# Two transformer blocks on one core: Pool's modulation sums in one block, a log-term buffer per head, spatial products between the z projections

## The chip, the core and the metric

The kernel runs on one core of a Trainium2 chip. Its engines are called here by the profile's names: PE (TensorE, the matrix unit; PEld its weight loads), DVE (VectorE), ACT (ScalarE), POOL (GpSimd) and SP (SyncE, which issues the weight loads from memory). The metric is the device time of one execution in microseconds, the median of several. Before the change it is 2369.49 us (three runs, 2369.08 to 2371.31).

## The reference

The program computes two transformer blocks in a row on 512 positions of width 1024, in float32. Only what the change touches:

```
c_act = silu(c);  mod = c_act @ w_ada + b_ada        # 9 vectors of 1024: 0,1,2 | 3,4,5 | 6,7,8
u = rmsnorm(x, g1) * (1 + mod[1]) + mod[0]           # first norm
h = x + 0.5 * mod[2] * swiglu(u)                     # FFN1, hidden width 2816
u = rmsnorm(h, g2) * (1 + mod[4]) + mod[3]           # second norm
y = mixer(u)      # short convolution, stick-breaking attention with 8 heads, gated merge, w_out
h = h + mod[5] * y
u = rmsnorm(h, g3) * (1 + mod[7]) + mod[6]           # third norm
h = h + 0.5 * mod[8] * swiglu(u)                     # FFN2, then a final norm

# stick-breaking attention, for each head and block of queries, strictly causal:
z = q @ k.T / 8;  sp = softplus(z);  rem = suffix sum of sp, without itself
a = exp(log_sigmoid(z) - rem);  o = a @ v

# second block, its spatial gating: 8 groups of 128 columns, 4 blocks of 128 positions
a = gelu(z_u) * (W_s[group] @ layernorm(gelu(z_v)) + b_s)
merged = gate_a * (a @ w_branch_a) + gate_b * (forgetting_attention @ w_branch_b)
```

## The kernel before

Activations stand transposed, as eight tiles of 128 features x 512 positions. Each operand of a dense product is split into a high part and a low rest, and each product is three matmuls (L448 high x high, L449 low x high, L450 high x low). A weight chunk is at most 8 tiles of 128 x 128: SP loads it into one of four slots (`raw`), ACT copies the high part (`split`, L837, `wh`), DVE subtracts to get the rest (`split`, L1216, `wl`), PE uses it (`dense`: 24 matmuls for 8 tiles). `split` runs three chunks ahead of PE, and SP reloads a slot when DVE has done its split. All engines run their own list of instructions in order; semaphores with counted values join them. The order of the lists is written out by hand.

**The modulation.** Vectors 0 and 1 are multiplied and added up by DVE itself at the start (L1582, L1586), PE sums over the partitions with a column of ones (L724, 32 pieces of one column, as a float32 product takes two passes), and DVE adds the bias (`modulation`, L1269) and makes the norm's gain (L1276). The other seven vectors are POOL's. For each vector it takes eight rows of tiles of `w_ada` through a ring of two buffers (`load`, L1774, 512 KB each, issued from POOL's own queue), multiplies by the column of `c_act` (L1786, L1788) and adds to `ada_acc` (L1792). There are only two accumulators, so POOL works in groups, each of which waits until PE has reduced the one before: vectors 2 and 3 after the first reduction, 4 and 5 after the first half of FFN1, 6 and 7 after the last head of the first attention (`o_lo`), since only then is the place free, and 8 after the reduction behind the output projection `out1`. `ada_reduce` on PE (L535) comes between the halves of FFN1 (2 and 3), after FFN1 (4 and 5), after `out1` (6 and 7) and between the halves of FFN2 (8).

**The norms.** PE sums squares with `mean_square` (L487), ACT takes the root, DVE inverts it (L1234), waits for the modulation, and then works tile by tile: DVE scales (L1252), ACT makes the high part (L867), DVE the rest (L1262), and PE starts a pair of dense products on each tile as it comes (`dense_pair`, 48 matmuls). FFN1 and FFN2 run in two halves (12 and 10 hidden tiles), each an up part (24 or 20 chunks of 8 tiles) and a down part (16 chunks of 6 or 5).

**The first attention** handles four pairs of heads (`body`, once per pair in each engine's list). For each head PE makes the scores z in PSUM (L546 to L549), and ACT three log terms into the buffer `x0`: |z| (L962), its exponential (L964) and the logarithm (L966). DVE makes the softplus (L1412), four suffix sums into `x1` (L1422) and the log weights back into `x0` (L1429), ACT the probabilities (L973). PE turns them (L558, `turn_probs`), ACT and DVE split them (L990, L1448, `turned_hi`, `turned_lo`), PE multiplies by the values (L573, L574). `x0` is shared by the two heads, so in ACT's list head 0's probabilities stand before head 1's log terms, which wait for them. Between these steps PE makes the projections of the next pair, and DVE's list has the weight splits, `q_lo` (L1360) and `k_lo` (L1367) of the next pair.

After it come four convolution tiles (`conv_in`, L1609 to L1621 on DVE), the merge (eight tiles, each two gates and two branches), and `out1`.

**The spatial gating of the second block** runs over eight groups m. DVE normalises the group (`normal_group`, L1672 to L1680), ACT and DVE split it (L1162, L1689), POOL masks the group's spatial weights, PE turns them (`turn_w`, L764) and makes 12 narrow matmuls (`mix_group`). DVE adds the bias (L1697) and multiplies with z (L1702), ACT and DVE split the result (L1167, L1704). PE also makes eight z projections (`z_in`, 24 matmuls), two of which fit in PSUM; ACT empties one (`z_out`, L1147) only when DVE has used the one two before, and `z_in` m waits for `z_out` m - 2. In PE's list `z_in(m + 4)` follows `mix_group(m)` for m = 0 to 3; the groups 4 to 6 follow with nothing between; then come the two gates of the merge's first tile and the last group:

```
            for m in range(DT - 1):
                turn_w(m + 1)
                mix_group(m // 4, m % 4)
                if m + 4 < DT:
                    z_in(m + 4)
```

Of the kernel before, what the change touches and what calls it, by code (L numbers as in the profile page):

```python
# [23 lines left out]
P = 128  # L24
# [56 lines left out]
def build(nc, a, out):  # L81
# [3 lines left out]
    with ctx:  # L85
# [58 lines left out]
        ada_acc = place("ada_acc", [P, 2 * D], F32, ada_at)  # L144
        ada_ring = place("ada_ring", [P, 4 * S], F32, ada_at + 4 * row)
# [23 lines left out]
        t1["x"] = place("x1", [P, 2 * PACK], F32, at)  # L169
        assert at + 8 * PACK <= ada_at  # L170
# [274 lines left out]
        def _(pe):  # L445
# [82 lines left out]
            def ada_reduce(group):  # L528

                count = 1 if group == 3 else 2  # L530

                pe.wait_ge(ada_add, 8 * (2 * group + count))
                for v in range(count):
                    for m in range(DT):
                        x = pe.matmul(bank(6, v * DT + m, 1), ada_acc[:, v * D + m * P:v * D + (m + 1) * P],  # L535
                                      one_col[:, :], start=True, stop=True, skip_group_check=True)
                x.then_inc(ada_red, 1)
# [116 lines left out]

            def merge(name, xa, xb, kt, ready_a, ready_b):
                nb, n0 = AT_[name], DT * ORDER[name]

                def gates(m):
                    for s, free in enumerate((MG["sa"], MG["sb"])):

                        pe.wait_ge(free, m + (n0 + 1))
                        if name == "merge2":
                            pe.wait_ge(G["z"], DT + 1 + s)
                        dense(nb + s, 4 * m, s, DT, uh, ul)
# [7 lines left out]
                gates(0)  # L672
                if name == "merge2":

                    mix_group(DT // 4 - 1, 3)
# [45 lines left out]
            pe.wait_ge(ada0, 16)  # L721
            for v in range(2):
                for m in range(DT):
                    mm = pe.matmul(bank(6, v * DT + m, 1), ada_acc[:, v * D + m * P:v * D + (m + 1) * P],  # L724
                                   one_col[:, :], start=True, stop=True, skip_group_check=True)
            mm.then_inc(ada_red, 1)

# [3 lines left out]
            ada_reduce(1)  # L731
# [17 lines left out]
            ada_reduce(2)  # L749
# [79 lines left out]
        def _(act):  # L829
# [79 lines left out]
            def attention(name, t, kind, pairs):  # L909
# [58 lines left out]
                def probabilities(p, hh):  # L968
                    pr = hh * PACK
                    if kind == 1:  # L970

                        act.wait_ge(A_["s_free"], 2 * p + (hh + 2))
                        act.activation(t["pr"][:, pr:pr + PACK], t["x"][:, 0:PACK], ACT.Exp).then_inc(A_["p"], 1)  # L973
# [236 lines left out]
        def _(dve):  # L1210
# [26 lines left out]
            def norm(q, k, gain, shift):  # L1237
# [27 lines left out]
            def modulation(n, v0, count):  # L1265
# [3 lines left out]
                dve.tensor_tensor(mods[:, v0 * DT:(v0 + count) * DT], bank(6, 0, count * DT),  # L1269
# [24 lines left out]
            def ffn(f, conv, gate):  # L1294
                s_, q, n0, r0 = F, RES_ROUND[f], FT * ORDER[f], DT * ORDER[f]
                for part, ((j0, tiles, kts), (gb, db)) in enumerate(zip(FFN_PARTS, chunks[f])):
# [37 lines left out]
                    if part == 0 and f == "ffn1":  # L1334
                        modulation(2, 2, 2)
                        half_gate(0, M_G0, 2)
                    if part == 0 and f == "ffn2":
                        modulation(5, 8, 1)
                        half_gate(2, M_G2, 5)
# [13 lines left out]
            def attention(name, t, kind, pairs):  # L1353
# [54 lines left out]
                def softplus(p, hh):  # L1408

                    x0, z = t["x"][:, 0:PACK], bank(B_HEAD[hh], 0, PACK)  # L1410
# [467 lines left out]
```

## Time and profile before

| | |
|---|---|
| median of three runs | 2369.49 us (2369.08 to 2371.31) |
| the profiled execution | 2372.86 us, its span 2371.2 us |
| PE busy | 2134.6 us, 90% of the span |
| DVE, ACT, POOL busy | 1305.7, 860.4, 308.2 us |
| mean granted PE clock | 0.937 of full speed |

The profile is of one execution. Times inside it count from the first instruction. PE's granted clock has two levels, 1.0 (2.4 GHz) and 0.5 (1.2 GHz), and a mean between them over a stretch is a mixture. Matmuls overlap: a dense matmul is shown with some 390 ns, but one follows the other every 227 to 235 ns at full clock and every 427 at half. Of POOL's times the page says that they are rough.

### The profile page before, as it was taken

The page shows a single profiled execution, that of the slowest core. Times are in us where ns is not written, and L with a number is a line of the kernel's source. Part 1 is how long each engine was busy: PE and PEld are TensorE (multiplying, and loading weights), DVE is VectorE, ACT ScalarE, POOL GpSimd, SP SyncE. Part 2 cuts the span into 40 slices and gives each one's busy share as a digit, 9 for nine tenths or more (in the row PEclk, how much of TensorE's full clock was granted, in tenths as well). Part 3 has the DMA queues.
Part 4 walks back from the last instruction along what each step waited for, and adds up shares of the span by engine and source line. Part 5 has one row for each costly group of instructions (what it writes and reads, how often), then busy time and mean ns, then how long its engine had stood idle before and what let it go on. Part 6 is the DMA issues. An engine that isn't in the chain of part 4 may idle for free.

```text
span 2371.2 us, 28854 instructions
## 1 busy us (share of the span) xinstructions
PE 2134.6 (90%) x9417; PEld 1752.2 (74%) x9417; DVE 1305.7 (55%) x1537; ACT 860.4 (36%) x1228; POOL 308.2 (13%) x222
## 2 busy tenths in 40 slices
PE   2799999887869997999996899997999989999967
PEld 2688888776647875888885688875788778888856
DVE  6844444666596448333346666666433466546554
ACT  2222223365414332222233556562222244334433
POOL 0843810000183006000000000011000000000000
PEclk6899999898879997999998899997899989999979
DMA  7453642221144333323323122233233322333212
GB/s 260 139 154 101 192 128 76 79 62 53 45 138 137 106 98 98 89 84 111 88 79 90 54 62 71 71 71 71 71 94 92 98 71 88 92 104 91 86 54 80
DMA packets 371706, 226.81 MB, mean 96 GB/s; under 512 B 8052, under 2 KB 361672, under 8 KB 370632
## 3 DMA queue, kind: packets, MB, share of 16 engines
q1 hardware_dynamic: 362248, 193.66, 27.8%
q0 software_dynamic: 9408, 32.51, 5.1%
q8 instruction: 28, 0.46, 0.1%
q14 instruction: 22, 0.18, 0.0%
HBM read 224.05 MB, written 2.10 MB: 95 GB/s over the span
## 4 chain that ended last, share of the span: by engine, by line
PE 80%; DVE 11%; ACT 4%; issue 4%; DVEq 0%; DMA 0%; ACTq 0%
PE ps L448 25%; PE ps L449 25%; PE ps L450 25%; DVE wl L1216 1%; PE ps L558 1%; DVE tmp L1252 1%; DVE x L1422 1%; PE ps L535 1%; DVE inv L1234 1%; PE ps L546 1%; PE ps L573 1%; PE ps L574 1%; PE ps L547 1%; DVE ssq L1229 1%; PE ps L487 1%
## 5 line engine op out<-in xcount | busy, mean ns | idle before, releaser
L448 PE MATMUL ps<-uh,wh 128*128 128x512 f32 x1896 | 764.2, 403 | 104.7 <-DVE ul L1262 36.7
L449 PE MATMUL ps<-ul,wh 128*128 128x512 f32 x1896 | 755.6, 399 | 0.0
L450 PE MATMUL ps<-uh,wl 128*128 128x512 f32 x1896 | 753.5, 397 | 0.0
L1216 DVE TENSOR_TENSOR wl<-raw,wh 128x1024 fp32r<-128x1024 f32 x389 | 531.2, 1369 | 248.2 <-ACT wh L837 240.5
L448 PEld LDWEIGHTS ps<-uh,wh 128*128 128x128 f32 x1896 | 366.8, 193 | 191.9 <-issue 63.5
L837 ACT ACTIVATE wh<-raw 128x1024 fp32r<-128x1024 f32 x389 | 408.7, 1052 | 223.3 <-PE ps L450 213.7
L450 PEld LDWEIGHTS ps<-uh,wl 128*128 128x128 f32 x1896 | 366.5, 193 | 79.1
L449 PEld LDWEIGHTS ps<-ul,wh 128*128 128x128 f32 x1896 | 367.0, 194 | 75.0
L448 PE MATMUL ps<-ah,wh 128*128 128x512 f32 x528 | 209.6, 397 | 0.0
L450 PE MATMUL ps<-ah,wl 128*128 128x512 f32 x528 | 209.2, 396 | 0.0
L449 PE MATMUL ps<-al,wh 128*128 128x512 f32 x528 | 209.1, 396 | 0.0
L1327 DVE TENSOR_TENSOR prod<-sq,ps 128x512 f32<-128x512 f32 x44 | 30.3, 688 | 278.2 <-PE ps L450 277.0
L1792 POOL TENSOR_TENSOR ada_acc<-ada_acc,ada_ring 128x1024 f32<-128x1024 f32 x49 | 138.9, 2835 | 3.8
L901 ACT ACTIVATE ah<-prod 128x512 f32 x66 | 41.8, 633 | 248.0 <-DVE prod L1327 248.0
L448 PEld LDWEIGHTS ps<-ah,wh 128*128 128x128 f32 x528 | 99.8, 189 | 23.9
L449 PEld LDWEIGHTS ps<-al,wh 128*128 128x128 f32 x528 | 99.8, 189 | 23.8
L450 PEld LDWEIGHTS ps<-ah,wl 128*128 128x128 f32 x528 | 99.7, 189 | 23.9
L1788 POOL TENSOR_TENSOR ada_ring<-ada_ring,cact 128x1024 f32<-128x1024 f32 x49 | 96.1, 1961 | 1.9 <-DMA ada_ring<-in_w_ada 0.9
L847 ACT ACTIVATE sq<-h 128x512 f32 x56 | 35.3, 631 | 158.6 <-DVE h L1292 89.4
L1786 POOL TENSOR_TENSOR ada_acc<-ada_ring,cact 128x1024 f32<-128x1024 f32 x7 | 13.7, 1951 | 598.3 <-DVE o1l L1504 336.7
L1851 POOL DMA_DIRECT2D ptok<-in_p x1 | 0.8, 807 | 626.7 <-DVE h L1290 626.7
L897 ACT ACTIVATE sq<-ps 128x512 f32<-128x512 f32 x44 | 26.3, 598 | 137.1 <-PE ps L450 137.1
(248 smaller groups left out, 2302.4 us busy)
## 6 DMA issues: line engine op xcount, KB each, us to landing
raw<-in_ffn_w_gu SPq DMA_DIRECT2D x88, 512.0 KB, 4.1
raw<-in_w_in SPq DMA_DIRECT2D x57, 512.0 KB, 3.8
ada_ring<-in_w_ada POOLq DMA_DIRECT2D x56, 512.0 KB, 4.1
raw<-in_w_up SPq DMA_DIRECT2D x44, 512.0 KB, 3.8
raw<-in_w_mix_in SPq DMA_DIRECT2D x40, 512.0 KB, 3.9
raw<-in_ffn_w_down SPq DMA_DIRECT2D x32, 384.0 KB, 3.2
raw<-in_ffn_w_down SPq DMA_DIRECT2D x32, 320.0 KB, 2.9
wada<-in_w_ada SPq DMA_DIRECT2D x8, 1024.0 KB, 12.7
```

Source lines behind the costliest of these rows:

```text
L448: pe.matmul(dst, lh, rh, start=first, stop=False, skip_group_check=True)
L449: pe.matmul(dst, lh, rl, start=False, stop=False, skip_group_check=True)
L450: return pe.matmul(dst, ll, rh, start=False, stop=last, skip_group_check=True)
L487: pe.matmul(bank(B_O), mean_w[:, :], ssq[:, :], start=True, stop=True).then_inc(ms_done, 1)
L837: act.activation(wh[:, w], raw[:, w], ACT.Copy).then_inc(w_hi, 1)
L847: act.activation(sq[:, r * S:(r + 1) * S], tile(h, m), ACT.Square).then_inc(sq_done, 1)
L897: act.activation(sq[:, buf], bank(2 * r), ACT.Silu).then_inc(s_["gate"], 1)
L901: act.activation(tile(ah, 2 * i + r), prod[:, buf], ACT.Copy).then_inc(s_["hi"], 1)
L1216: dve.tensor_tensor(wl[:, w], raw[:, w], wh[:, w].bitcast(F32), ALU.subtract).then_inc(w_lo, 1)
L1327: dve.tensor_tensor(prod[:, buf], factors[0], factors[1], ALU.mult).then_inc(s_["prod"], 1)
L1788: pool.tensor_tensor(ring[r], ring[r], w, ALU.mult).then_inc(ada_mul, 1)
L1792: pool.tensor_tensor(acc, acc, ring[r], ALU.add).then_inc(ada_add, 1)
```

## The change

Three edits that do not depend on each other.

1. *Modulation.* Each vector has its own place (`ada_homes`; some lie where other stages keep their tiles later, and are reduced before that), the ring lies elsewhere, and POOL runs all seven vectors in one loop without groups. It starts when the first norm is done (`u_ready`), and vector 5 waits for the first reduction, whose place it takes. PE reduces vector 2 between the halves of FFN1, vectors 3 and 4 and then 5 after FFN1, and 6, 7 and 8 after `out1`; nothing is reduced in FFN2. DVE takes vector 5's modulation after the second norm, and vector 8's half gate goes to the third.
2. *First attention.* Three buffers instead of two: one `x0` per head, and `x1`. ACT no longer waits for the other head's probabilities; head 1's log terms stand before head 0's probabilities. In DVE's list one weight split moves behind head 1's log weights.
3. *Spatial products.* `z_in(m + 3)` follows `mix_group(m)` for m = 1 to 4, and the first two gates of the merge follow groups 5 and 6.

```
-        ada_acc = place("ada_acc", [P, 2 * D], F32, ada_at)
-        ada_ring = place("ada_ring", [P, 4 * S], F32, ada_at + 4 * row)
+        ada_ring = place("ada_ring", [P, 4 * S], F32, rows(32))
+        ada_homes = (ada_at, ada_at + 2 * row, rows(36), rows(26), rows(28),
+                     ada_at, ada_at + 2 * row, ada_at + 4 * row, ada_at + 6 * row)
+        ada_acc = [place(f"ada_acc{v}", [P, D], F32, x) for v, x in enumerate(ada_homes)]
-        t1["x"] = place("x1", [P, 2 * PACK], F32, at)
+        t1["x"] = place("x1", [P, 3 * PACK], F32, at)
...
                     if f == "ffn1" and part == 0:
-                        ada_reduce(0)
-                    if f == "ffn2" and part == 0:
-                        ada_reduce(3)
+                        ada_reduce((2,))
...
+            def ada_reduce(vs):
+                if vs[0] == 0:
+                    pe.wait_ge(ada0, 16)
+                else:
+                    pe.wait_ge(ada_add, 8 * (vs[-1] - 1 if vs[-1] < 5 else 7))
+                for v in vs:
                     for m in range(DT):
+                        x = pe.matmul(bank(5 if v == 5 else 6, v * DT + m, 1), ada_acc[v][:, m * P:(m + 1) * P],
                                       one_col[:, :], start=True, stop=True, skip_group_check=True)
                 x.then_inc(ada_red, 1)
...
             mean_square(1)
-            ada_reduce(1)
+            ada_reduce((3, 4))
+            ada_reduce((5,))
...
             mean_square(2)
-            ada_reduce(2)
+            ada_reduce((6, 7, 8))
...
-            for m in range(DT - 1):
-                turn_w(m + 1)
+            for m in range(DT):
+                if m + 1 < DT:
+                    turn_w(m + 1)
                 mix_group(m // 4, m % 4)
-                if m + 4 < DT:
-                    z_in(m + 4)
+                if 1 <= m < 5:
+                    z_in(m + 3)
+                elif 5 <= m < 7:
+                    merge_gate("merge2", 0, m - 5)
...
                 def log_terms(p, hh):
-                    x0 = t["x"][:, 0:PACK]
+                    x0 = t["x"][:, hh * PACK:(hh + 1) * PACK]
                     act.wait_ge(A_["s"], 2 * p + (hh + 1))
-                    act.wait_ge(A_["p"], 2 * p + (hh + 1))
...
+                    soft(p, 1)
                     if kind == 1:
                         probabilities(p, 0)
-                    soft(p, 1)
...
                 if q == 1:
-                    modulation(3, 4, 2)
+                    modulation(3, 3, 2)
                     gain_of(1, C_N2, 3)
                 if q == 2:
-                    modulation(4, 6, 2)
+                    modulation(5, 6, 3)
                     gain_of(2, C_N3, 4)
+                    half_gate(2, M_G2, 5)
...
                         q_lo(p + 1)
-                        split(nb + 4 + LEAD, it)
                     turned_lo(p, 0)
                     if kind == 1:
                         log_weights(p, 1)
+                    if not last:
+                        split(nb + 4 + LEAD, it)
...
             norm(1, 1, (gains, DT), 3 * DT)
+            modulation(4, 5, 1)
...
+            def load(n):
+                k, v = n % DT, 2 + n // DT
+                pool.dma_start(ring[n % 2], a["w_ada"][0, k * P:(k + 1) * P, v * D:(v + 1) * D]).then_inc(ada_ld[n % 2], 16)
+            load(0)
+            load(1)
+            pool.wait_ge(u_ready, 2 + 8)
+            for v in range(2, 9):
+                acc = ada_acc[v][:, :]
+                if v == 5:
+                    pool.wait_ge(ada_red, 1)
                 for k in range(DT):
...
+                    if n + 2 < 7 * DT:
+                        pool.wait_ge(ada_add, n + 1)
+                        load(n + 2)
```

## Rows read from the trace of the kernel before

**Rows 1.** The page's chain that ended last, share of the span by engine.
```profile
PE 80%; DVE 11%; ACT 4%; issue 4%; DVEq 0%; DMA 0%; ACTq 0%
```

**Rows 2.** By stretch, three norms: length; PE, PEld, DVE, ACT, POOL busy (count); clock, DMA, GB/s.
```profile
55.80:90.00 34.20, 17.80 (x48) 12.13 (x49) 32.07 (x19) 8.21 (x11) 29.55 (x18) 0.71 0.32 89
460.00:476.40 16.40, 12.97 (x48) 10.61 (x49) 12.60 (x20) 6.07 (x9) 0.00 (x0) 0.75 0.01 1
893.10:929.05 35.95, 19.35 (x48) 13.45 (x49) 33.98 (x19) 8.60 (x11) 32.01 (x19) 0.64 0.30 88
```

**Rows 3.** Table by stretch: convolution and first merge tiles, merge, FFN1 beside POOL.
```profile
641.40:740.00 98.60, 73.91 (x293) 58.86 (x292) 89.30 (x49) 25.50 (x32) 81.20 (x46) 0.88 0.48 138
740.00:840.00 100.00, 100.00 (x438) 81.90 (x438) 47.17 (x51) 35.50 (x42) 0.00 (x0) 1.00 0.39 112
90.00:146.00 56.00, 56.00 (x249) 46.39 (x248) 41.16 (x22) 17.29 (x23) 49.01 (x28) 1.00 0.66 196
```

**Rows 4.** DVE groups, 90 to 146: count | busy, mean ns | idle before, releaser.
```profile
L1216 DVE TENSOR_TENSOR wl<-raw,wh 128x1024 fp32r<-128x1024 f32 x11 | 27.4, 2494 | 0.1
L1327 DVE TENSOR_TENSOR prod<-sq,ps 128x512 f32<-128x512 f32 x6 | 4.1, 688 | 15.4 <-PE ps L450 14.2 <-ACT sq L897 1.2
```

**Rows 5.** DVE groups, 308 to 386, without POOL.
```profile
L1216 DVE TENSOR_TENSOR wl<-raw,wh 128x1024 fp32r<-128x1024 f32 x15 | 18.3, 1221 | 0.1
```

**Rows 6.** PE's order of time: start, length; the reduction before the third norm.
```profile
886.97 5.97 PE L535 MATMUL ps<-one_col,ada_acc 128*128 128x1 f32 x32
```

**Rows 7.** Table by stretch: reductions inside FFN1 and FFN2, and behind each.
```profile
209.80:214.40 4.60, 4.60 (x33) 4.56 (x32) 2.42 (x3) 1.58 (x2) 0.00 (x0) 0.75 0.21 62
214.40:219.00 4.60, 4.60 (x13) 3.64 (x13) 2.96 (x3) 0.00 (x0) 3.39 (x3) 0.51 0.14 31
1048.90:1050.60 1.70, 1.70 (x17) 1.67 (x15) 1.38 (x2) 0.56 (x2) 0.00 (x0) 1.00 0.00 0
1050.60:1055.20 4.60, 4.60 (x22) 3.77 (x22) 2.52 (x5) 1.13 (x3) 0.00 (x0) 1.00 0.35 101
```

**Rows 8.** POOL's order of time: first and last of the second group's 16 steps.
```profile
214.92 1.89 POOL L1786 TENSOR_TENSOR ada_acc<-ada_ring,cact 128x1024 f32<-128x1024 f32 x1 [67.69 <-PE ps L535]
...
307.11 0.59 POOL L1774 DMA_DIRECT2D ada_ring<-in_w_ada  x1 [0.64 <-POOL ada_acc L1792]
```

**Rows 9.** DVE's order of time, one attention pair; in brackets idle before, releaser.
```profile
536.23 1.22 DVE L1216 TENSOR_TENSOR wl<-raw,wh 128x1024 fp32r<-128x1024 f32 x1
541.69 1.49 DVE L1412 SCALAR_TENSOR_TENSOR x<-ps,x 128x1280 f32<-128x1280 f32 x1 [4.25 <-ACT x L966]
...
547.50 1.23 DVE L1216 TENSOR_TENSOR wl<-raw,wh 128x1024 fp32r<-128x1024 f32 x1
...
550.29 1.48 DVE L1429 TENSOR_TENSOR x<-ps,x 128x1280 f32<-128x1280 f32 x1
```

**Rows 10.** PE's order of time, the same pair: the transposes of both heads.
```profile
537.67 1.31 PE L558 MATMUL ps<-ident,a_pr 128*128 128x128 f32 x10 [0.56 <-ACT a_pr L973]
...
553.13 2.40 PE L558 MATMUL ps<-ident,a_pr 128*128 128x128 f32 x10 [0.92 <-ACT a_pr L973]
```

**Rows 11.** ACT's order of time, the same pair: head 0's probabilities.
```profile
536.34 1.27 ACT L973 ACTIVATE a_pr<-x 128x1280 f32<-128x1280 f32 x1 [4.78 <-DVE x L1429]
```

**Rows 12.** DVE's order of time, spatial groups 0 to 1.
```profile
1598.99 1.22 DVE L1216 TENSOR_TENSOR wl<-raw,wh 128x1024 fp32r<-128x1024 f32 x1 [0.26 <-ACT wh L837]
...
1606.91 1.22 DVE L1216 TENSOR_TENSOR wl<-raw,wh 128x1024 fp32r<-128x1024 f32 x1
...
1615.38 0.69 DVE L1697 TENSOR_TENSOR ssq<-ps,gsm 128x512 f32<-128x512 f32 x1 [4.70 <-PE ps L450]
```

**Rows 13.** Chain of waits, 1598 to 1690: start, length, what.
```profile
1605.30 0.79 PE ps L448
1606.09 0.43 PE ps L449
...
1679.83 0.70 DVE ssq L1697
```

More of the change, by code:

```diff
@@ L653, in attention, with merge_gate @@
                 body(pairs - 1, True)
+            def merge_gate(name, m, s):
+                pe.wait_ge((MG["sa"], MG["sb"])[s], m + (DT * ORDER[name] + 1))
+                if name == "merge2":
+                    pe.wait_ge(G["z"], DT + 1 + s)
+                dense(AT_[name] + s, 4 * m, s, DT, uh, ul)
             def merge(name, xa, xb, kt, ready_a, ready_b):
@@ L658, in gates @@
                 def gates(m):
[L659 to L664, printed above, removed]
+                    for s in range(2):
+                        merge_gate(name, m, s)
                 def branches(m):
@@ L719, in _ @@
             mean_square(0)
[L721 to L726, printed above, removed]
+            ada_reduce((0, 1))
             ffn("ffn1", False)
             mean_square(1)
-            ada_reduce(1)
+            ada_reduce((3, 4))
+            ada_reduce((5,))
             pe.wait_ge(setup_r, 4)
@@ L972, in probabilities @@
                         act.wait_ge(A_["s_free"], 2 * p + (hh + 2))
[L973 removed]
+                        act.activation(t["pr"][:, pr:pr + PACK], t["x"][:, pr:pr + PACK], ACT.Exp).then_inc(A_["p"], 1)
                     else:
@@ L1334, in ffn @@
                     if part == 0 and f == "ffn1":
-                        modulation(2, 2, 2)
+                        modulation(2, 2, 1)
                         half_gate(0, M_G0, 2)
-                    if part == 0 and f == "ffn2":
-                        modulation(5, 8, 1)
-                        half_gate(2, M_G2, 5)
                     if part == 1:
@@ L1408, in softplus @@
                 def softplus(p, hh):
-                    x0, z = t["x"][:, 0:PACK], bank(B_HEAD[hh], 0, PACK)
+                    x0, z = t["x"][:, hh * PACK:(hh + 1) * PACK], bank(B_HEAD[hh], 0, PACK)
                     dve.wait_ge(A_["ln"], 2 * p + (hh + 1))
@@ L1416, in suffix_sums @@
                     g1 = 2 * p + (hh + 1)
-                    x0, x1 = t["x"][:, 0:PACK], t["x"][:, PACK:2 * PACK]
+                    x0, x1 = (t["x"][:, x * PACK:(x + 1) * PACK] for x in (hh, 2))
                     dve.wait_ge(A_["sp"], g1)
@@ L1425, in log_weights @@
                 def log_weights(p, hh):
-                    x0, x1, z = t["x"][:, 0:PACK], t["x"][:, PACK:2 * PACK], bank(B_HEAD[hh], 0, PACK)
+                    x0, x1 = (t["x"][:, x * PACK:(x + 1) * PACK] for x in (hh, 2))
+                    z = bank(B_HEAD[hh], 0, PACK)
                     dve.wait_ge(A_["c"], 2 * p + (hh + 1))
@@ L1771, in _ @@
             ring = [ada_ring[:, r * D:(r + 1) * D] for r in range(2)]
-            def load(k, r, col):
-                pool.dma_start(ring[r], a["w_ada"][0, k * P:(k + 1) * P, bass.ds(col, D)] if not isinstance(col, int)
-                               else a["w_ada"][0, k * P:(k + 1) * P, col:col + D]).then_inc(ada_ld[r], 16)
-            def vector(v, it, slot, last):
-                acc = slot
+            def load(n):
[5 more added lines that the diff above has]
+            for v in range(2, 9):
+                acc = ada_acc[v][:, :]
+                if v == 5:
+                    pool.wait_ge(ada_red, 1)
                 for k in range(DT):
@@ L1788, in vector @@
                         pool.tensor_tensor(ring[r], ring[r], w, ALU.mult).then_inc(ada_mul, 1)
-                        pool.wait_ge(ada_mul, 7 * (v - 2) + k + 7 * it)
-                        pool.wait_ge(ada_add, n + 8 * it)
+                        pool.wait_ge(ada_mul, 7 * (v - 2) + k)
+                        pool.wait_ge(ada_add, n)
                         pool.tensor_tensor(acc, acc, ring[r], ALU.add).then_inc(ada_add, 1)
-                    if not (last and k >= DT - 2):
-                        pool.wait_ge(setup, 1)
-                        pool.wait_ge(ada_add, n + 1 + 8 * it)
-                        k2 = (k + 2) % DT
-                        load(k2, r, (v + (k + 2) // DT) * D + it * D)
-            load(0, 0, 2 * D)
-            load(1, 1, 2 * D)
-            with pool.Fori(0, 2) as group:
-                pool.wait_ge(setup, 1)
-                pool.wait_ge(ada_red, group + 1)
-                for x in range(2):
-                    vector(2 + x, 2 * group, ada_acc[:, x * D:(x + 1) * D], False)
-            pool.wait_ge(A["att1"]["o_lo"], 1 + 4)
-            pool.wait_ge(ada_red, 3)
-            for x in range(2):
-                vector(2 + x, 4, ada_acc[:, x * D:(x + 1) * D], False)
-            pool.wait_ge(ada_red, 4)
-            vector(8, 0, ada_acc[:, 0:D], True)
+                    if n + 2 < 7 * DT:
+                        pool.wait_ge(ada_add, n + 1)
+                        load(n + 2)
             pool.wait_ge(h_new, 2 + 8 * 4)
```

18 lines of the change are left out of this document (6 added, 12 removed).

## The prediction

> **What bounds the kernel now.** I read the chain of waits first [rows 1]: four fifths of it is TensorE (PE), and nearly all of that is the dense products. A microsecond is therefore won only where PE stands or runs at its lower clock, and the table by stretch shows where. Between the moment a modulation is known and the 48th matmul behind it the first norm takes 34.2 us, the third 35.95, the second 16.4, with identical work [rows 2]; POOL is busy in the two slow ones and idle in the quick one. From the first convolution to the second tile of the merge PE issues 293 pieces in 98.6 us with POOL busy for 81.2, and 438 in the next 100 us without it [rows 3]. In the first feed-forward block (FFN1) POOL is as busy, 196 GB/s flow, and PE is full at clock 1.00 [rows 3]. So POOL's sums cost time where VectorE (DVE) is on the path, and none where DVE has slack. The DVE rows say why: beside POOL the weight split (L1216, both inputs in SBUF) means 2494 ns, without it 1221 [rows 4, 5]; the product of L1327, with one input in PSUM, stays at 688.
>
> By the Trainium skill ("SBUF — State Buffer", section "Who interferes with whom") a VectorE instruction with two SBUF inputs and a GpSimd instruction that reads SBUF exclude each other for the whole instruction, and whoever starts first wins. The trace agrees as far as the 2494 against 1221 ns goes. The rule speaks against this change in one place, FFN1, and is a rival below.
>
> **Part 1, Pool in one block.** All seven sums (2 to 8) now run from the end of the first norm.
>
> *First norm.* POOL's arithmetic no longer overlaps it, so I give it the second norm's time: 34.2 - 16.4 = 17.8 us [rows 2]. Upper end the same; lower end 12, if the first POOL steps catch the last norm tiles.
>
> *Convolution and merge.* Without POOL a convolution tile costs DVE two splits of 1.22 us [rows 5] and five 512-wide operations of about 0.7 (an estimate from L1327's 688 ns), with the trip through ScalarE (ACT) some 7 us; PE needs 48 pieces, 48 x 100/438 = 11 us. PE becomes the bound: 293 x 100/438 = 66.9 us against 98.6, a gain of 31.7 [rows 3]. I take 31, lower end 16 (half, if some wait of DVE for PE stays).
>
> *Third norm.* 35.95 - 16.4 = 19.55 us [rows 2]. Against it, three vectors are reduced there instead of two: 32 pieces took 5.97 us [rows 6], so 16 more are 3.0 (1.7 at full clock [rows 7]). All three vectors' modulation is one DVE instruction as before; a half gate adds 0.4. Net 16.1, ends 12 and 17.5.
>
> *Reductions between the halves of FFN1 and FFN2.* Two vectors cost 4.6 us, and the 4.6 us behind them ran at clock 0.51 with 13 pieces [rows 7]. One vector in FFN2 cost 1.7, and the next 4.6 us held 22 pieces at clock 1.00. FFN1 now has one vector: 2.9 + 9 pieces of 0.21 us = 4.8 (ends 2.9 and 5). FFN2 has none: 1.7.
>
> *Vector 5 reduced behind 3 and 4.* 16 pieces, 1.7 to 3.0 us [rows 6, 7], while PE would anyway stand until the norm's first tile, which in the second norm comes about 3.5 us after the modulation (of 16.4 us PE was busy 12.97 [rows 2]). Cover of 3.4 us for at most 3.0: nothing. Without that cover it costs 3. Its modulation on DVE comes after the norm, ahead of work that waits for PE: nothing.
>
> *POOL's queue.* 16 steps took 214.92 to 307.7, 5.80 us each [rows 8]. The block starts near 70 (55.8 plus most of 16.4), and 56 steps end near 395. PE asks for the last sum when FFN1 is over: 460.0 minus the reduction and the gains before it, near 437. Slack 42 us. Of the 56 loads of 512 KB 24 move from the convolution and the third norm into FFN1, where [rows 3] show the traffic of weights and ring together leave PE full. What POOL issues afterwards (the forget bias, the masks) waits for later residuals either way.
>
> *FFN1 under POOL.* The up halves keep slack: 2 x 2.49 + 2.4 + 0.7 = 8.1 us of DVE for 11 of PE. New is the second down half, 240 pieces of 0.23 us that end some 11 us (square sum, reduction) before 437, so from near 371 to POOL's end at 395: per output tile PE has 30 pieces, 6.9 us, and DVE two splits (2.49 each), a residual (about 0.75) and a square sum that can be held like a split (2.4), 8.1 us. Worst case 1.2 us on four tiles, 5 lost; best none. I take 1.5.
>
> **Part 2, the log-term buffer per head.** Before, head 1's three log terms waited for head 0's probabilities, which left DVE idle for 4.25 us ahead of the second softplus [rows 9]. Now they run while DVE does head 0's sums, the softplus follows the split of 536.23, and the 4.25 us go. The split at 547.50 (1.23 us [rows 9]) moves behind the log weights. Head 1's probabilities thus come 5.5 us earlier per pair; the transposes behind them took 2.40 us after the idle time against 1.31 for head 0's [rows 10], so up to 1.1 more comes back with the clock. What is late next is PE itself, then the probabilities of head 1, by my estimate 1.5 us after the values of head 0. ACT had stood 4.78 us before head 0's probabilities [rows 11]; the three log terms, each like the 1.27 us of that exponential, are 3.9 and fit. Three full pairs at 6.3 (between 5.5 and 6.9) and the last at 4.2 (no split moved): 23. If the log terms did not fit, head 0's probabilities would be late by up to 3.9 us in four pairs, a loss of 16; the upper end is 27.
>
> **Part 3, spatial products between z projections.** Before, the z projection behind group m waited for the tile that ACT frees after that same group, so PE stood and DVE in turn waited 4.70 us for PE [rows 12]; then three groups ran with no dense product between. Now a projection or gate is issued whose bank was freed a group earlier. DVE's own cycle, where nothing waited, is 1606.91 - 1598.99 = 7.92 us [rows 12]; PE's is 24 + 12 narrow pieces, 5.5 + 1.8 = 7.3. So DVE sets the pace: from 1606.9 five cycles of 8.0, a last one of 6.2 without split, then the last product 2 to 3: group 7 is ready near 1656 in place of 1679.83 [rows 13], 24 us. After the first group PE now stands 5 us, so the first projection runs partly at the lower clock, as the one at 1605.30 did (its pieces 0.43 us apart [rows 13] instead of 0.23); I take 1 off: 23. Lower end a loss of 10 (PE at the low clock throughout: 6 x 13 us), upper 30 (PE full).
>
> **Sum.** 17.8 + 31 + 16.1 + 4.8 + 1.7 - 1.5 + 23 + 23 = 115.9 us. The profiled execution took 2372.86 us (span 2371.2), so 2257.0 by its own time; the median of the runs shown, 2369.49, is 3.4 lower, so the forecast is **2254 us**.
>
> **Rivals.**
> *The lock in FFN1* (the rule above): DVE sets FFN1's pace in more than four tiles because POOL itself is held by DVE and takes 6.4 us a step, ending near 428. Eight tiles at 1.2: 10 us in place of 1.5, 2262. For it: 8.1 against 6.9 us. Against it: steps of 5.80 with DVE just as loaded.
> *The low clock eats parts 2 and 3*: short stops of 1 to 5 us stay in each pair and group, and PE runs slow behind them, as the 2.40 us of [rows 10] and the projection of [rows 13] show: parts 2 and 3 give 15 and 14, 2271.
> *Another wait takes the place of head 0's probabilities* in part 2 (ACT's copies of the next query, which now stand behind them): nothing gained there, 2277. Against it: DVE's idle 4.25 us has ACT's logarithm as its only releaser.
> *The convolution stays DVE-bound*: half of 31 is kept, 2269.
> *Slower: POOL is too late.* If a step took longer than (437 - 70)/56 = 6.6 us, PE would stand at the reduction of vector 5, 5.6 us for each further 0.1. The 116 us are gone at (437 + 116 - 70)/56 = 8.6 us a step; at 9 the time would be 2254 + 56 x (9 - 6.6) = 2388. For it: the block crosses stretches of dense DVE work. Against it: 5.80 us [rows 8], and 81.2 us busy in 98.6 even where DVE was busiest [rows 3].
>
> **How the numbers follow.** Forecast 0.68 (its own range 2244 to 2264), lock 0.07, low clock 0.10, convolution 0.06, pair 0.05, POOL late 0.02, something unnamed 0.02 (split evenly over no change and slower). The range reaches from the upper ends of the terms that have room (parts 2 and 3, some 11 us together: 2242) over the low clock and the pair to 2282. A measurement of this kernel tells 0.2% (4.7 us) from no change; only POOL's lateness and half of the unnamed give slower (0.03), the other half no change (0.01).
>
> **What would show it.** In the profile after: 48 matmuls within 17 us in all three norms, the third 20 counting its reduction; POOL busy in one stretch from about 70 to 395 and idle after it; from the first convolution on, PE at 438 pieces per 100 us; pairs of the first attention 6 to 7 us closer together; the spatial groups about 8 us apart; no idle PE at the end of FFN1 other than the norm's. The prediction is wrong if POOL ends after 437, if DVE still waits for ACT's logarithm of head 1, or if FFN1 up to its last residual takes longer than before by more than 5 us beyond its norm.

## The result and the profile after

The changed kernel takes 2248.16 us (median of 4 runs, 2247.28 to 2253.92) against 2369.28 us in the same call (2368.79 to 2371.31): a ratio of 0.9492, 95% interval 0.9476 to 0.9509, or 121.1 us less. The forecast was 2254, and its range reached from 2242 to 2282. The profiled execution took 2248.09 us, 124.8 less than the profiled one of before, which lay 3.6 us above its median. One execution of loads_without_sums, below, took 11956.62 us; it is left out, and that kernel's time is the median of the three others.

Three lines of the page of after: busy time by engine, POOL by slice, and the chain that ended last.
```profile
PE 2093.9 (93%) x9417; PEld 1727.0 (77%) x9417; DVE 1285.9 (57%) x1537; ACT 861.1 (38%) x1228; POOL 310.5 (14%) x222
...
POOL 0799996000000000000000000021000000000000
...
PE 86%; DVE 8%; ACT 3%; issue 2%; DMA 0%; DVEq 0%; ACTq 0%; POOL 0%
```
POOL's sums are one block at the front, and PE holds 86% of the chain where it held 80 [rows 1].

The table by stretch of after, columns as in [rows 2]: first norm; FFN1 beside POOL; the 4.6 us behind FFN1's reduction; second norm; one attention pair, from head 0's transposes to the next pair's; convolution and first merge tiles; merge; third norm; spatial groups.
```profile
54.80:71.40 16.60, 13.13 (x48) 10.66 (x49) 12.95 (x19) 8.08 (x11) 2.90 (x3) 0.75 0.07 21
90.00:146.00 56.00, 56.00 (x249) 46.37 (x248) 43.32 (x21) 15.65 (x20) 51.37 (x30) 1.00 0.64 189
193.00:197.60 4.60, 4.60 (x22) 3.77 (x22) 4.57 (x4) 1.12 (x3) 4.50 (x3) 1.00 0.66 195
439.00:451.30 12.30, 12.23 (x48) 10.01 (x49) 10.14 (x16) 4.62 (x7) 0.00 (x0) 0.87 0.01 1
505.53:538.86 33.33, 30.94 (x161) 26.14 (x161) 24.96 (x32) 23.62 (x32) 0.00 (x0) 1.00 0.22 63
590.90:657.80 66.90, 66.07 (x291) 54.11 (x290) 40.38 (x50) 25.77 (x32) 0.00 (x0) 1.00 0.32 92
657.80:757.80 100.00, 100.00 (x438) 81.98 (x437) 46.47 (x50) 35.53 (x42) 0.00 (x0) 1.00 0.35 102
815.90:832.90 17.00, 13.21 (x50) 10.71 (x51) 13.04 (x20) 8.35 (x11) 0.00 (x0) 0.75 0.00 0
1502.80:1557.00 54.20, 47.72 (x247) 40.18 (x246) 44.31 (x81) 16.87 (x32) 11.87 (x22) 0.94 0.37 78
```
Of before, the same view for two of these, the attention pair and the spatial groups:
```profile
537.67:578.31 40.64, 34.09 (x160) 28.62 (x160) 25.15 (x31) 23.60 (x31) 0.00 (x0) 0.87 0.18 52
1600.40:1679.50 79.10, 58.94 (x247) 48.92 (x246) 44.88 (x82) 16.83 (x32) 11.85 (x22) 0.76 0.25 54
```
All three norms now issue their matmuls in 12.3 to 17 us [rows 2]. The stretch of the convolution needs 66.9 us for 291 pieces where it took 98.6 for 293 [rows 3]. An attention pair is 7.31 us shorter with the same matmuls (160 or 161 by where the stretch ends), the spatial groups 24.9. FFN1 stays full beside a POOL that is busier than before.

POOL's order of time in after: the first steps and the last sum.
```profile
68.18 1.90 POOL L1793 TENSOR_TENSOR ada_acc<-ada_ring,cact 128x1024 f32<-128x1024 f32 x1 [50.45 <-DVE ul L1263]
70.37 0.59 POOL L1776 DMA_DIRECT2D ada_ring<-in_w_ada  x1 [0.30 <-POOL ada_acc L1793]
...
372.90 2.73 POOL L1799 TENSOR_TENSOR ada_acc<-ada_acc,ada_ring 128x1024 f32<-128x1024 f32 x1
```
The block runs from 68.18 to 375.63: 56 steps of 5.49 us where [rows 8] had 5.80. Its gap ahead of a load is 0.30 us, before it was 0.64.

PE's order of time in after: the reductions (L537) in FFN1, ahead of the second and of the third norm, with what follows; between them the transposes (L560) of both heads of a pair.
```profile
191.28 1.84 PE L537 MATMUL ps<-one_col,ada_acc 128*128 128x1 f32 x16
192.99 0.48 PE L451 MATMUL ps<-ah,wh 128*128 128x512 f32 x1
...
427.62 1.25 PE L490 MATMUL ps<-ssq,mean_w 128*128 128x512 f32 x2 [2.65 <-DVE ssq L1229]
428.67 10.24 PE L537 MATMUL ps<-one_col,ada_acc 128*128 128x1 f32 x48
439.06 0.77 PE L451 MATMUL ps<-uh,wh 128*128 128x512 f32 x1 [0.16 <-DVE ul L1263]
...
505.53 1.31 PE L560 MATMUL ps<-ident,a_pr 128*128 128x128 f32 x10 [0.57 <-ACT a_pr L973]
515.39 1.31 PE L560 MATMUL ps<-ident,a_pr 128*128 128x128 f32 x10 [1.83 <-ACT a_pr L973]
...
804.10 2.08 PE L490 MATMUL ps<-ssq,mean_w 128*128 128x512 f32 x2 [2.64 <-DVE ssq L1229]
805.96 10.24 PE L537 MATMUL ps<-one_col,ada_acc 128*128 128x1 f32 x48
819.99 0.76 PE L451 MATMUL ps<-uh,wh 128*128 128x512 f32 x1 [3.79 <-DVE ul L1263]
```
Two things are to be seen. Ahead of the second norm the reduction of vector 5 fills PE's wait for the norm (0.16 us idle); ahead of the third, where vectors 6 to 8 come at once, PE stands 3.79 us. And head 1's transposes follow head 0's by 9.86 us, where they came 15.46 behind and took 2.40 us [rows 10].

DVE's order of time in after: the pair's splits and head 1's softplus, then splits of two spatial groups and the last group.
```profile
504.09 1.22 DVE L1216 TENSOR_TENSOR wl<-raw,wh 128x1024 fp32r<-128x1024 f32 x1
505.22 1.48 DVE L1410 SCALAR_TENSOR_TENSOR x<-ps,x 128x1280 f32<-128x1280 f32 x1
...
513.96 1.21 DVE L1216 TENSOR_TENSOR wl<-raw,wh 128x1024 fp32r<-128x1024 f32 x1
...
1509.22 1.23 DVE L1216 TENSOR_TENSOR wl<-raw,wh 128x1024 fp32r<-128x1024 f32 x1
1517.13 1.23 DVE L1216 TENSOR_TENSOR wl<-raw,wh 128x1024 fp32r<-128x1024 f32 x1
...
1557.32 0.69 DVE L1698 TENSOR_TENSOR ssq<-ps,gsm 128x512 f32<-128x512 f32 x1 [2.30 <-PE ps L453]
```
The 4.25 us of idle time ahead of the softplus [rows 9] are gone, and the split stands behind the log weights. The spatial groups follow each other in DVE's own cycle, 7.91 us, the length that one group had before without a wait [rows 12].

### The profile page after: what moved, and what is told of

The parts are those of the page before. It is cut to its first block, busy times and chain, and to the rows that moved or that the text cites. A ratio compares the mean times of both kernels' runs of the same rounds, so it can differ in the third digit from the quotient of the medians.

```text
span 2246.3 us, 28669 instructions
## 1 busy us (share of the span) xinstructions
PE 2093.9 (93%) x9417; PEld 1727.0 (77%) x9417; DVE 1285.9 (57%) x1537; ACT 861.1 (38%) x1228; POOL 310.5 (14%) x222
## 4 chain that ended last, share of the span: by engine, by line
PE 86%; DVE 8%; ACT 3%; issue 2%; DMA 0%; DVEq 0%; ACTq 0%; POOL 0%
PE ps L451 27%; PE ps L452 27%; PE ps L453 27%; PE ps L537 1%; PE ps L560 1%; DVE x L1420 1%; DVE inv L1234 1%; PE ps L548 1%; DVE wl L1216 1%; PE ps L575 1%; PE ps L576 1%; PE ps L549 1%; DVE ssq L1229 1%; DVE x L1410 1%; PE ps L490 0%
## 5 line engine op out<-in xcount | busy, mean ns | idle before, releaser
L451 PE MATMUL ps<-uh,wh 128*128 128x512 f32 x1896 | 750.4, 396 | 40.1 <-DVE pxl L1717 14.8
L452 PE MATMUL ps<-ul,wh 128*128 128x512 f32 x1896 | 744.4, 393 | 0.0
L453 PE MATMUL ps<-uh,wl 128*128 128x512 f32 x1896 | 743.9, 392 | 0.0
L1216 DVE TENSOR_TENSOR wl<-raw,wh 128x1024 fp32r<-128x1024 f32 x389 | 547.4, 1409 | 250.3 <-ACT wh L838 242.9
L451 PEld LDWEIGHTS ps<-uh,wh 128*128 128x128 f32 x1896 | 360.1, 190 | 117.7 <-issue 28.4
L453 PEld LDWEIGHTS ps<-uh,wl 128*128 128x128 f32 x1896 | 359.7, 190 | 76.4
L452 PEld LDWEIGHTS ps<-ul,wh 128*128 128x128 f32 x1896 | 360.4, 190 | 73.6
L1333 DVE TENSOR_TENSOR al<-prod,ah 128x512 f32 x66 | 86.1, 1305 | 20.4 <-ACT ah L902 20.4
```

What stands on the lines that cost most here:

```text
L451: pe.matmul(dst, lh, rh, start=first, stop=False, skip_group_check=True)
L452: pe.matmul(dst, lh, rl, start=False, stop=False, skip_group_check=True)
L453: return pe.matmul(dst, ll, rh, start=False, stop=last, skip_group_check=True)
L1216: dve.tensor_tensor(wl[:, w], raw[:, w], wh[:, w].bitcast(F32), ALU.subtract).then_inc(w_lo, 1)
L1333: dve.tensor_tensor(tile(al, 2 * i + r), prod[:, buf], tile(ah, 2 * i + r).bitcast(F32), ALU.subtract).then_inc(s_["lo"], 1)
```

## The experiments

**The three parts alone.** Each kernel is the one of before with one part of the change. The core of each:
```diff
 pool_alone
+            load(0)
+            load(1)
+            pool.wait_ge(u_ready, 2 + 8)
+            for v in range(2, 9):
 heads_alone
-                    x0 = t["x"][:, 0:PACK]
+                    x0 = t["x"][:, hh * PACK:(hh + 1) * PACK]
 spatial_alone
+                if 1 <= m < 5:
+                    z_in(m + 3)
+                elif 5 <= m < 7:
+                    merge_gate("merge2", 0, m - 5)
```


> The kernel before with part 1 alone (Pool in one block, reductions moved). Theory: the three parts do not touch one another, and part 1 is worth what the two traces show at its places, about 18 us at the first norm, 5 at the first reduction, 1.5 at the second norm, 31 at convolution and merge, 14 at the third norm, 1.5 in FFN2: 71 us, 2298 us (2292 to 2304). Rival: the parts overlap (the attention's earlier end only pays because POOL is gone, or the reverse): the three gains measured alone sum to less than 110 or more than 132.

> The kernel before with part 2 alone (log-term buffer per head, the split moved). Theory of independent parts: 25 us, 2344 us (2340 to 2350), PE's stop ahead of head 0's values gone. Rival: with POOL still starting behind the last head, the convolution eats part of it: 2350 or more.

> The kernel before with part 3 alone (z projections and gates one group later). Theory of independent parts: 25 us, 2344 us (2340 to 2349), the groups 8 us apart as in the kernel with all parts. Rival: DVE's cycle has room only because of something in the other parts: under 20 us.

Measured: 2301.39 us (ratio 0.9714, 0.9698 to 0.9730), 2346.32 (0.9900, 0.9882 to 0.9918) and 2343.75 (0.9892, 0.9876 to 0.9909), with 2369.12 before. That is 67.7, 22.8 and 25.4 us, 115.9 together; the whole change gave 121.1. The 5.2 us between lie within the intervals, which are some 4 us to either side for each kernel. All three came out in their ranges: the parts do not need each other. What the whole attention gained in heads_alone (24.2 us in the trace) also answers the rival by which another wait takes the old one's place.

**loads_without_sums.** The kernel before with POOL's loads kept, but its sums one column wide, except for the first multiplication of each vector; vectors 2 to 8 of the modulation are not computed. The semaphore updates at the ends of the lines are left out here.
```diff
-pool.tensor_tensor(ring[r], ring[r], w, ALU.mult)
+pool.tensor_tensor(ring[r][:, 0:1], ring[r][:, 0:1], cact[:, k:k + 1], ALU.mult)
-pool.tensor_tensor(acc, acc, ring[r], ALU.add)
+pool.tensor_tensor(acc[:, 0:1], acc[:, 0:1], ring[r][:, 0:1], ALU.add)
```


> The kernel before, with POOL's loads and their order kept, but of each step after the first of a vector only one column multiplied and added (the modulation vectors 2 to 8 are therefore not computed). Theory: POOL's wide instructions hold DVE's two-input instructions; without them the first and third norm take the second one's 16 to 17 us for 48 matmuls, the convolution and merge 293 pieces in about 67 us, and the time is 2369 - 18 - 18 - 31 = 2302 us (2296 to 2308). Rival: it is the traffic of the ring's loads; they are all still there, closer together, so the norms stay above 30 us and the time above 2355.

Measured: 2305.19 us, ratio 0.9728 (0.9708 to 0.9747), within the expected range. The table by stretch for its first norm:
```profile
55.00:72.50 17.50, 12.84 (x48) 10.40 (x49) 13.80 (x19) 7.89 (x11) 8.94 (x17) 0.74 0.57 161
```
More traffic than before flows beside this norm (161 GB/s, in [rows 2] 89), and it takes 17.5 us. Between the same matmuls as in the table further below, this kernel gained 16.7 us at the first norm, 30.0 at convolution and merge and 16.9 at the third norm. What held DVE in all three was POOL's arithmetic and not its loads.

**longer_steps.** The changed kernel, with one more full multiplication (by 1) in 49 of the 56 steps; the waits and the semaphore update that belong to it are left out here.
```diff
+pool.tensor_tensor(ring[r], ring[r], one_col[:, 0:1].to_broadcast([P, D]), ALU.mult)
```


> The kernel after, with one more full-width multiplication (by one) in 49 of POOL's 56 steps, some 2 us each. POOL ended at 375.6 us and PE asks for vector 5 near 435.5. Theory of a hard slack: POOL now ends between 474 and 488, PE stands at the reduction of vector 5 until then, FFN1 itself ends as before (sum of squares at 428 +- 2), 2248 + 40 to 52 us: 2288 to 2300. Rival (the hold also sets FFN1's pace): the second down half, now wholly beside POOL, needs 8.1 us of DVE per tile against 6.9 of PE, and the sum of squares comes near 437 us.

Measured: 2310.59 us, ratio 0.9755 (0.9739 to 0.9771), 62 more than the changed kernel. PE's order of time at the end of FFN1:
```profile
443.00 2.07 PE L490 MATMUL ps<-ssq,mean_w 128*128 128x512 f32 x2 [10.33 <-DVE ssq L1229]
444.87 6.83 PE L537 MATMUL ps<-one_col,ada_acc 128*128 128x1 f32 x32
493.23 3.57 PE L537 MATMUL ps<-one_col,ada_acc 128*128 128x1 f32 x16 [41.54 <-POOL ada_acc L1801]
```
DVE's groups, 380 to 443, where POOL now still works:
```profile
L1216 DVE TENSOR_TENSOR wl<-raw,wh 128x1024 fp32r<-128x1024 f32 x15 | 45.1, 3042 | 1.0 <-ACT wh L838 0.7
```
The forecast missed, in two places. POOL ended at 493.2, later than the 474 to 488 expected, and PE, whose queue holds the reduction of vector 5 ahead of the second norm, stood 41.5 us: the mechanism of the prediction's slower case, at its place. That reduction waits for all 56 steps (`8 * 7` in `ada_reduce`) and not for vector 5 alone, whose sum was done at 311.5: until POOL is done its ring lies in the place where the attention has its `x1`. And the rival named for this run holds too: the mean square behind FFN1 came 15.4 us late (443.00 against 427.62), since a split took 3042 ns in the second down half, 0.69 to 0.75 us went to each square sum, and DVE needed some 8.5 us for an output tile, where the tiles of the changed kernel follow each other every 7.0. Ahead of that half PE stayed full, 82.0 of the 82 us from 68 to 150 and 107.0 of the 107 from 193 to 300.

**sum_beside_norm, one_gap_wait, four_gap_waits.** The first is the changed kernel in which POOL begins with vector 2 beside the first norm, as before the change. The others add to this one or four waits for an event long past ahead of each load; the kernel before had one such wait there, which the change had dropped.
```diff
 sum_beside_norm
-            pool.wait_ge(u_ready, 2 + 8)
+            pool.wait_ge(ada_red, 1)
+                if v == 3:
+                    pool.wait_ge(u_ready, 2 + 8)
 one_gap_wait (four_gap_waits: four of them)
+                        pool.wait_ge(setup, 1)
                         pool.wait_ge(ada_add, n + 1)
                         load(n + 2)
```


> The kernel after, but POOL's vector 2 starts when the first reduction is done, beside the first norm, as before the change (vectors 3 to 8 still wait for the norm's end). Theory of the hold by POOL's arithmetic: the first norm goes back to some 34 us for its 48 matmuls, 16 to 18 us lost, 2265 us (2262 to 2268). Rival: the first norm got faster because the reduction and the start moved or the loads are fewer: under 5 us lost.

> The kernel of sum_beside_norm (vector 2 summed by POOL beside the first norm) with one wait for an event long past put ahead of each of POOL's loads, which lengthens POOL's gap there and changes nothing else. Theory: what made that norm 30 us longer and not 17 is POOL's gap before a load, 0.30 us where the kernel before had 0.64; with a gap of 0.4 to 0.6 us DVE gets a second operation into some of the steps, the norm's 48 matmuls end near 90 to 97 (101.8 without the wait) and the time is 2269 to 2276 us (2281 without). Rival, the gap is not the cause: the matmuls still end at 101 or later, as POOL's steps are longer, and the time is 2280 to 2284.

> As one_gap_wait with four such waits ahead of each load. Theory (the gap decides how many of DVE's operations fit into one of POOL's steps): a gap of 0.6 us or more, the first norm's 48 matmuls end at 90 or before, the time 2262 to 2270 us. Rival, the gap is not the cause: they end at 101 or later and the time is 2280 us or more.

Measured: 2281.25 us (0.9632, 0.9617 to 0.9646), 2269.65 (0.9586, 0.9570 to 0.9602) and 2270.05 (0.9590, 0.9574 to 0.9606). The first cost 33 us where 16 to 18 were expected; its 48 matmuls end at 101.8 us, with one wait at 92.2, with four at 91.1, in the changed kernel at 71.4. DVE's order of time in sum_beside_norm, then POOL's beside it:
```profile
57.65 5.72 DVE L1253 SCALAR_TENSOR_TENSOR tmp<-h,gains,inv 128x512 f32<-128x512 f32 x2 [0.38 <-DVE gains L1277]
63.30 5.67 DVE L1263 SCALAR_TENSOR_TENSOR ul<-tmp,mods,uh 128x512 f32 x2
```
```profile
68.72 0.59 POOL L1776 DMA_DIRECT2D ada_ring<-in_w_ada  x1 [0.30 <-POOL ada_acc L1801]
69.33 1.91 POOL L1797 TENSOR_TENSOR ada_ring<-ada_ring,cact 128x1024 f32<-128x1024 f32 x1
71.32 2.68 POOL L1801 TENSOR_TENSOR ada_acc<-ada_acc,ada_ring 128x1024 f32<-128x1024 f32 x1
```
The same two views of one_gap_wait:
```profile
57.83 3.24 DVE L1253 SCALAR_TENSOR_TENSOR tmp<-h,gains,inv 128x512 f32<-128x512 f32 x2 [0.38 <-DVE gains L1277]
60.99 3.49 DVE L1263 SCALAR_TENSOR_TENSOR ul<-tmp,mods,uh 128x512 f32 x2
64.40 5.29 DVE L1253 SCALAR_TENSOR_TENSOR tmp<-h,gains,inv 128x512 f32<-128x512 f32 x2
```
```profile
63.82 0.59 POOL L1776 DMA_DIRECT2D ada_ring<-in_w_ada  x1 [0.56 <-POOL ada_acc L1801]
```
With a gap of 0.30 us every two operations of DVE last one step of POOL, 5.7 us; with 0.56 some take 3.2 to 3.5. So POOL's gap decides, while its loads are the same: a wait that waits for nothing made the whole some 11 us faster. Four waits lengthened the gap to 0.58 us only, below the 0.6 expected, and gave nothing more; the matmuls' end and the time lie just above what was expected for them.

**split_kept.** The changed kernel with the second split where it was, ahead of head 1's log weights (the first line below is on that place).
```diff
+                        split(nb + 4 + LEAD, it)
-                    if not last:
-                        split(nb + 4 + LEAD, it)
```


> The kernel after without the move of one weight split behind head 1's log weights in the first attention. Theory: the split's 1.23 us is on the path of three of four pairs, 3.5 us lost, with the clock behind it up to 6: 2252 to 2254 us. Rival: PE sets the pair's length, the split is hidden: no change, 2248.

Measured: 2256.94 us, ratio 0.9535 (0.9522 to 0.9548), 8.8 more than the changed kernel; 4 to 6 were expected. PE's order of time in it, at the values of head 0 and behind head 1's transposes:
```profile
516.12 0.50 PE L575 MATMUL ps<-a_pth,a_vv 128*128 128x512 f32 x1 [0.73 <-DVE a_ptl L1447]
...
519.75 1.31 PE L560 MATMUL ps<-ident,a_pr 128*128 128x128 f32 x10 [1.96 <-ACT a_pr L973]
520.82 0.58 PE L451 MATMUL ps<-uh,wh 128*128 128x512 f32 x1
...
521.62 0.63 PE L453 MATMUL ps<-uh,wl 128*128 128x512 f32 x1
522.05 0.63 PE L451 MATMUL ps<-uh,wh 128*128 128x512 f32 x1
```
And in the changed kernel at the same place:
```profile
516.77 0.39 PE L452 MATMUL ps<-ul,wh 128*128 128x512 f32 x1
517.00 0.40 PE L453 MATMUL ps<-uh,wl 128*128 128x512 f32 x1
```
A pair is 2.83 us longer (36.15 between the same operation, L1365, of two pairs, 33.32 in the changed kernel). The split is 1.23 of it. The rest is for the most part clock: with another stop, of 0.73 us ahead of the values, and then one of 1.96, the matmuls behind the transposes came 0.43 us apart, the lower level, instead of 0.23. The first ten took 3.96 us and in the changed kernel 2.40. There the one stop of 1.83 us, with none ahead of the values, left the clock up.

**two_more_waits, ple_wait_late, vector8_late.** The second block ends with its own feed-forward (FFN3) and a last stage that adds a product of an embedding behind one more norm (PLE in the kernel). The profile after shows PE idle for 3.79 us at the third norm and 14.84 us ahead of the PLE stage. The first kernel shortens both waits of the changed kernel, the others one each. With vector 8 reduced by itself, DVE takes its modulation after the third norm, which the cut below does not show.
```diff
 ple_wait_late
-            pe.wait_ge(PL["lo"], 2)
             ...
             dense_pair(nb, (0, 2), DT, uh, ul, u_at(5))
             ...
+            pe.wait_ge(PL["lo"], 2)
 vector8_late
-            ada_reduce((6, 7, 8))
+            ada_reduce((6, 7))
+            ada_reduce((8,))
```


> The kernel after with two more waits shortened. One: in the last stage PE waited 14.84 us for both low parts of the embedding, which DVE makes after the whole norm, before it began the first pair of dense products; the wait moves behind that pair, so that PE waits only for the norm's first tile, as after the other norms (7 us): 8 us gained. Two: vector 8 is reduced behind 6 and 7, as vector 5 is behind 3 and 4, and its modulation follows the third norm: 16 pieces at the low clock, 3 us gained. Theory: 11 us, 2237 us (2234 to 2240). Rival: the first pair now runs tile by tile at the low clock and gives back half: 2242.

> The changed kernel with only the wait of the PLE stage moved behind the matmuls that do not read what it waits for. If the two parts of two_more_waits add, this one is worth the 12.4 us that are left when 3.5 are taken from 15.8: 2234 to 2238 us. Rival, part of that came from the clock being full after both stages together: 2239 to 2242.

> The changed kernel with only vector 8 reduced separately, behind vectors 6 and 7. By the third norm of two_more_waits 3.5 us: 2243 to 2246 us. Rival: the time is taken again at the next wait and stays at 2247 to 2249.

Measured: 2232.34 us (0.9433, 0.9420 to 0.9446), 2238.49 (0.9454, 0.9439 to 0.9470) and 2245.17 (0.9485, 0.9469 to 0.9501). The first is the fastest kernel of this study: 15.8 us under the changed one by the medians, 14.0 by the two ratios, where 11 were expected. vector8_late came out in its range, but it can't be told from the changed kernel by its time (the intervals overlap); its third norm is 3.7 us shorter in the trace. PE's order of time at the PLE stage, first of after, then of ple_wait_late, and at the third norm of vector8_late:
```profile
2170.17 0.80 PE L451 MATMUL ps<-uh,wh 128*128 128x512 f32 x1 [14.84 <-DVE pxl L1717]
```
```profile
2164.32 0.77 PE L451 MATMUL ps<-uh,wh 128*128 128x512 f32 x1 [4.14 <-DVE ul L1261]
```
```profile
818.90 0.76 PE L451 MATMUL ps<-uh,wh 128*128 128x512 f32 x1 [0.16 <-DVE ul L1263]
```
The stop at the PLE stage fell from 14.84 to 4.14 us, and the stage with its 48 matmuls by 11.6 in ple_wait_late and 12.8 in two_more_waits. 8 had been expected; the 10.7 us of idle time themselves were the better estimate. ple_wait_late lies just above its range of 2234 to 2238. Two of its four runs are within it, at 2235.56 and 2236.05. The profiled one is not, at 2241.43; in it four stages that the edit does not touch ran 0.7 to 1.6 us longer than in the changed kernel (last section).

## Why the prediction was right, step by step

Each stage measured between the starts of the same matmul in the profiled executions of before and after, in us:

| step | predicted | measured |
|---|---|---|
| first norm | 17.8 | 17.6 |
| reduction in FFN1, less FFN1 beside POOL | 4.8 - 1.5 | 5.0 |
| second norm, vector 5 | 0 | 1.5 |
| first attention | 23 | 25.5 |
| convolution and merge | 31 | 31.3 |
| third norm | 16.1 | 14.2 |
| reduction in FFN2 | 1.7 | 1.6 |
| spatial groups | 23 | 24.8 |
| start and the last two norms, not touched | 0 | 3.3 |
| sum | 115.9 | 124.8 |

The stages that the change touches gained 121.5 us in this pair of executions. Four terms were 1.5 to 2.5 us too low and the third norm 1.9 too high; none is off by more. (The range's lower end is 2243 by its own terms, 2254 less 11, and not 2242; nothing hangs on it.) None of the signs of being wrong came: POOL ended at 375.6, DVE's softplus follows the split without a wait, and FFN1 became shorter.

*First norm, convolution, both reductions.* Right to within 0.3 us, and for the reason given: loads_without_sums shows that it is POOL's arithmetic, and the convolution's 291 pieces run at the merge's rate. One vector's reduction took 1.84 us, and the 4.6 us behind it hold 22 pieces at clock 1.00 where two vectors left 13 at 0.51 [rows 7].

*FFN1 beside POOL.* The loss of 1.5 did not come. POOL was 20 us earlier than the 395 that I worked out (the shorter gap), so it met hardly any of the second down half. That this half would be held by DVE where POOL works beside it, as I said, shows in longer_steps, though with three operations in a step of POOL where the changed kernel has two. The tile of DVE was 8.5 us where I had 8.1, but made up otherwise: a split took 3042 ns, where I took 2494 from the up half [rows 4], and the square sum, which I let be held like a split (2.4), mostly 0.7. The rival of the lock is thus wrong for this kernel, where a step shrank to 5.49 us, and right as a mechanism where POOL reaches further. The lateness of POOL as the slower case needs more than 6.6 us a step by the prediction, with 5.6 us for each further 0.1; at 7.58 (425 us for 56 steps in longer_steps) that is 55, and the kernel lost 62 (41.5 of it the stop, 15.4 FFN1).

*Vector 5 at nothing.* Right: PE stands 0.16 us ahead of the norm's first matmul, its wait is filled. The 1.5 us measured there are not the step's: ple_wait_late, vector8_late and pool_alone have the same norm and gained between -0.1 and 0.0 (last section).

*Third norm.* The one term that was too large. A further vector was put at 3.0 us; 48 pieces took 10.24 us against 5.97 for 32 [rows 6], so 4.3. PE was at its lower clock already at the mean square ahead of them (2.08 us for two matmuls, 1.12 before), another 1.0. That level, and not the vector, was the error: in pool_alone, where the mean square took 1.13 us, the 48 pieces took 8.84, so 2.9 for the further vector, and the term was 15.8 against 16.1. Why the stage is reached at the lower level with all three parts was not tried. The 48 matmuls came within 17 us; "20 counting its reduction" counted the added vector only, the whole is 26.9.

*Attention.* A pair is 7.31 us shorter, not 6.3. The 4.25, the split and the transposes make 6.6; the rest goes with the clock, 0.87 before and 1.00 after over a pair: the old stop took the products behind it to the lower level too. (heads_alone and six others with this edit gained 23.9 to 24.2 in the whole stage, two_more_waits 25.2.) The rival by which the low clock eats parts 2 and 3 had the wrong sign: fewer stops gave more than their own length.

*Spatial groups.* DVE sets the pace at 7.91 us, the last group is ready at 1557.3. The stages ahead had gained 97.7, so that is 1655.0 in the time of before, against 1656 worked out. Taking 1 us off for the clock was not needed.

## What to carry to other kernels

When DVE works on two SBUF inputs, place POOL's arithmetic beside a stretch where PE is full and DVE has slack, and price it by the stretch that it leaves, at the rate that PE reaches without it. A stop of PE can be worth more than its length, when the matmuls behind it run at the lower level, as in split_kept; the one of 1.83 us in the changed kernel was not. And look in each profile for a wait that stands in an engine's queue ahead of work that does not need it; the two found here were worth some 15 us more.

## What the runs showed of the hardware that I had not expected

*A shorter gap in POOL's work can make DVE slower.* Beside steps with a gap of 0.30 us the first norm's matmuls ended at 101.8 us, with 0.56 us at 92.2. That norm is a run of DVE's two-input operations; the splits of FFN1 do not show the gap. Their mean was 1221 ns alone, 2494 beside the steps of before [rows 4, 5] and 2690 beside those of after, but 2668 in four_gap_waits with its gap of 0.58 us, in the same stretch, and 2462 in after from 300 to 375. DVE's groups of after, 90 to 146:
```profile
L1216 DVE TENSOR_TENSOR wl<-raw,wh 128x1024 fp32r<-128x1024 f32 x11 | 29.6, 2690 | 0.0
...
L1328 DVE TENSOR_TENSOR prod<-sq,ps 128x512 f32<-128x512 f32 x5 | 3.4, 687 | 11.6 <-PE ps L453 11.6
```
With the gap of 0.30 us DVE got one operation in for each of POOL's; with the longer one, by its shorter pairs, sometimes a second. The Trainium skill ("SBUF — State Buffer", section "Who interferes with whom") says that the engine that issues first keeps the shared ports for its whole instruction; the trace agrees, with two operations of DVE in 5.67 us beside a step of two operations in 5.58. The operation that reads one input from PSUM took 687 ns beside POOL; in the kernel before it took 688 both beside POOL [rows 4] and without it (308 to 386).

*A norm with the same instructions has two lengths.* From the mean square to the 48th matmul behind it, the second norm gained, against before, 1.56 to 1.58 us in sum_beside_norm, split_kept, two_more_waits and both kernels with added waits, 1.5 in the changed kernel, and -0.1 to 0.0 in pool_alone, ple_wait_late and vector8_late, all with the same edit there (in longer_steps PE stands there for POOL). The norm ahead of FFN3, which no edit touches, gained 1.4 to 1.6 in six of the thirteen kernels (the changed one among them) and 0.0 to 0.1 in the other seven. The clock granted over 12.3 us from the second norm's first dense matmul was 0.87 in the changed kernel and in split_kept, and 0.75, 0.81 and 0.80 in pool_alone, vector8_late and ple_wait_late. When within a norm PE's clock rises thus seems to fall in one of two places; what decides it was not tried. Such steps in the two norms, and differences of 0.7 and 1.3 us in the spatial groups and the attention, are why the profiled execution of ple_wait_late lies above the range, and they hide 3.7 us of vector8_late in the whole time.
